# A PEER trunk kernel on one core: a group's one-hots in two VectorE instructions, two dots in front of them in every group, one set of dots beside each retrieval

## The reference, cut to what matters

```python
q = (hc @ wq).reshape(t, 8, 2, 128)
s = einsum("thpk,pnk->thpn", q, sk)                 # scores against 2 x 128 keys
s1, i1 = top_k(s[:, :, 0], 16); s2, i2 = top_k(s[:, :, 1], 16)
best, j = top_k(s1[..., :, None] + s2[..., None, :], 16)
e = i1[j // 16] * 128 + i2[j % 16]
gate = softmax(best)
act = gelu(einsum("thkd,td->thk", u_tab[e], hc))
out = einsum("thk,thkd->td", gate * act, v_tab[e])
```

## Time and profile before

| | us |
|---|---|
| median of 3 runs | 3139.86 (3136.67 to 3146.48) |
| profiled execution | 3141.54 |
| its span, first to last instruction | 3139.8 |
| busy: TensorE, VectorE | 2904.3 (93%), 2430.9 (77%) |
| busy: ScalarE, GpSimd | 1207.3 (38%), 1424.9 (45%) |
| mean granted TensorE clock | 0.975 of full |

### The profile page before, as it was taken

How to read it: one execution, slowest core, us unless ns; L and a number is a source line. 1 busy time by engine, 2 the same in 40 slices (tenths; PEclk the granted TensorE clock), 3 DMA queues, 4 the chain that set the end, 5 groups by cost and what they waited for, 6 DMA issues and landing times.

```text
span 3139.8 us, 50852 instructions
## 1 busy us (share of the span) xinstructions
PE 2904.3 (93%) x15754; PEld 2554.2 (81%) x15754; DVE 2430.9 (77%) x4532; ACT 1207.3 (38%) x1590; POOL 1424.9 (45%) x878
## 2 busy tenths in 40 slices
PE   5888999999998899999899899999999989999997
PEld 3657999989888788888777689989888878888885
DVE  7965679999995688888765307799999937888887
ACT  2333333345553333333333324333555523333332
POOL 2623367776667122222324244777766651222221
PEclk8999999999999999999999899999999989999998
DMA  6336567779898899999935124777788898999996
GB/s 240 134 128 221 199 206 240 242 263 349 308 350 321 301 353 350 355 356 352 351 122 174 66 100 138 229 251 239 277 328 328 310 348 308 352 353 351 357 347 232
DMA packets 352434, 849.74 MB, mean 271 GB/s; under 512 B 30048, under 2 KB 194016, under 8 KB 350176
## 3 DMA queue, kind: packets, MB, share of 16 engines
q1 hardware_dynamic: 239888, 479.53, 44.5%
q0 software_dynamic: 73728, 268.47, 23.6%
q10 hardware_dynamic: 38736, 100.84, 8.1%
HBM read 741.76 MB, written 106.95 MB: 270 GB/s over the span
## 4 chain that ended last, share of the span: by engine, by line
PE 54%; DVE 21%; issue 11%; POOL 7%; DMA 4%; ACT 1%; SPq 0%; POOLq 0%; DVEq 0%; ACTq 0%
PE bank L1418 11%; PE bank L1419 11%; PE bank L1420 11%; POOL w_lo L407 6%; DVE oh_c L995 5%; DVE oh_j L999 5%; PE bank L1360 4%; PE bank L1362 4%; PE bank L1361 4%; DVE rows L1160 2%; PE bank L1260 2%; PE bank L1262 2%; PE bank L1261 2%; DVE oh_i L996 2%; DMA x<-u_rows,u_idx 1%
## 5 line engine op out<-in xcount | busy, mean ns | idle before, releaser
L407 POOL TENSOR_TENSOR w_lo<-w_raw,w_hi 128x1024 fp32r<-128x1024 f32 x338 | 838.6, 2481 | 694.1 <-ACT w_hi L517 692.2
L517 ACT ACTIVATE w_hi<-w_raw 128x1024 fp32r<-128x1024 f32 x594 | 629.1, 1059 | 1346.3 <-PE bank L1420 668.6
L1360 PE MATMUL bank<-h_hi,w_hi 128*128 128x384 f32 x2048 | 702.7, 343 | 42.5 <-POOL w_lo L407 29.8
L1362 PE MATMUL bank<-h_lo,w_hi 128*128 128x384 f32 x2048 | 688.9, 336 | 0.0
L1361 PE MATMUL bank<-h_hi,w_lo 128*128 128x384 f32 x2048 | 688.3, 336 | 0.0
L461 POOL DMA_INDIRECT shared<-stream,v_idx x256 | 246.8, 964 | 830.9 <-DVE rows L1069 746.6
L1418 PE MATMUL bank<-w_hi,h_hi 128*128 128x512 f32 x1536 | 600.7, 391 | 16.6 <-ACT h_hi L642 14.3
L1419 PE MATMUL bank<-w_hi,h_lo 128*128 128x512 f32 x1536 | 600.0, 391 | 0.0
L1420 PE MATMUL bank<-w_lo,h_hi 128*128 128x512 f32 x1536 | 599.8, 390 | 0.0
L1039 DVE TENSOR_TENSOR w_lo<-w_raw,w_hi 128x1024 fp32r<-128x1024 f32 x256 | 313.7, 1226 | 199.9 <-ACT w_hi L517 199.0
L1360 PEld LDWEIGHTS bank<-h_hi,w_hi 128*128 128x128 f32 x2048 | 387.1, 189 | 58.9 <-issue 55.9
(11 more groups left out here) (193 smaller groups left out, 3584.6 us busy)
## 6 DMA issues: line engine op xcount, KB each, us to landing
w_raw<-stream SPq DMA_DIRECT2D x600, 512.0 KB
act_dram<-act_words ACTq DMA_DIRECT2D x256, 192.0 KB
gate_dram<-shared ACTq DMA_DIRECT2D x12, 4096.0 KB, 16.1
act_words<-act_dram SPq DMA_DIRECT2D x256, 192.0 KB
shared<-gate_dram SPq DMA_DIRECT2D x128, 384.0 KB
oh_j<-mod_rows SPq DMA_DIRECT2D x60, 512.0 KB, 4.7
oh_i<-mod_rows SPq DMA_DIRECT2D x20, 512.0 KB, 5.4
shared<-mod_rows SPq DMA_DIRECT2D x16, 512.0 KB, 14.0
```

Of the source, the lines that this page charges most:

```text
L407: nc.gpsimd.tensor_tensor(lo_of(grp, s), w_raw[:, s, :], hi_of(grp, s).bitcast(F32), ALU.subtract).then_inc(S["lo_ready"], 1)
L517: nc.scalar.activation(hi_of(grp, s), w_raw[:, s, :], ACT.Copy).then_inc(S["hi_ready"], 1)
L1360: MM(o, hi, h_hi[:, k, P:T], start=(k == 0), stop=False)
L1362: ins = MM(o, hi, h_lo[:, k, P:T], start=False, stop=(k == KC - 1))
```

## The change

It merges the two comparisons of a group into one instruction (`oh_i` and `oh_c` now lie in one tensor `oh_ic`, the keys of a group side by side in `keys_t`), and the three products into another (`gate_p` by group). In every group two dots come first, then the one-hots. The retrieval blocks keep the set of dots at their end and lose the other. GpSimd's fetch schedule follows: one fetch a tile for six tiles of a block; dots_to(g) changes from 36 + g + (g + 1) // 2 to 18 + 2g, and 14 dots are left behind the groups instead of 20.

```diff
-EARLY = 2 * DB * EARLY_SET
+EARLY = DB * EARLY_SET
 def dots_to(g):
-    return EARLY + g + (g + 1) // 2
+    return EARLY + 2 * g
...
-        oh_i = sb("oh_i", [P, 2, PAIR, NK, 2], BF16)
-        oh_c = sb("oh_c", [P, PAIR, NK, 2], BF16)
+        oh_ic = sb("oh_ic", [P, 3, PAIR, NK, 2], BF16)
+        oh_i, oh_c = oh_ic[:, 0:2, :, :, :], oh_ic[:, 2, :, :, :]
...
-        gate_p = key_words[:, 0:3 * DT].rearrange("p (a b) -> p a b", a=3)
-        i_t = key_words[:, 3 * DT:4 * DT]
-        j_t = key_words[:, 4 * DT:5 * DT]
+        gate_p = key_words[:, 0:3 * DT].rearrange("p (g w t) -> p g w t", w=3, t=GROUP)
+        keys_t = key_words[:, 3 * DT:5 * DT].rearrange("p (g w t) -> p g w t", w=2, t=GROUP)
...
                     if b < TB:
-                        end = 2 * (b - 1) * EARLY_SET + min(max(r - 1, 0), EARLY_SET) + (
-                            EARLY_SET if r == TILES_PER_BLOCK - 1 else max(r - 10, 0))
+                        end = (b - 1) * EARLY_SET + min(max(r - 2, 0), EARLY_SET)
                     elif group < GROUPS:
                         end = min(dots_to(max(group - 1, 0)) + U_RING, n + 2)
...
-                def early_dots(b, half):
+                def early_dots(b):
...
-                    early_dots(b, 0)
...
-                    V.tensor_copy(i_t[:, bass.ds(at, P)], ps[4][:, 0:P])
-                    V.tensor_copy(j_t[:, bass.ds(at, P)], ps[4][:, P:2 * P])
+                    for w in range(2):
+                        V.tensor_copy(keys_t[:, bass.ds((b - 1) * (P // GROUP), P // GROUP), w, :],
+                                      ps[4][:, w * P:(w + 1) * P].rearrange("p (g t) -> p g t", t=GROUP))
...
-                    early_dots(b, 1)
+                    early_dots(b)
...
                 def of_group(t, g):
-                    return t[:, g * GROUP:(g + 1) * GROUP].rearrange("p (a b) -> p a b", b=2).unsqueeze(2
-                                                                     ).to_broadcast([P, PAIR, NK, 2])
+                    n = t.shape[2]
+                    return t[:, g, :, :].rearrange("p n (a b) -> p (n a) b", b=2).unsqueeze(2
+                                                                   ).to_broadcast([P, n * PAIR, NK, 2])
                 def one_hots(g):
                     s = g % 2
-                    keys = iota_2[:].unsqueeze(1).to_broadcast([P, PAIR, NK, 2])
+                    keys = iota_2[:].unsqueeze(1).to_broadcast([P, 2 * PAIR, NK, 2])
...
-                    V.tensor_tensor(oh_c[:], keys, of_group(j_t, g), ALU.is_equal).then_inc(S["oh_cmp"], 1)
-                    V.tensor_tensor(oh_i[:, s, :, :, :], keys, of_group(i_t, g), ALU.is_equal)
+                    V.tensor_tensor(oh_ic[:, s:3:2 - s, :, :, :], keys, of_group(keys_t, g), ALU.is_equal
+                                    ).then_inc(S["oh_cmp"], 1)
                     dve.wait_ge(S["oh_cmp"], groups + g + 1)
-                    for w in range(3):
-                        ins = V.tensor_tensor(oh_j[:, s, w, :, :, :], oh_c[:], of_group(gate_p[:, w, :], g), ALU.mult)
-                    ins.then_inc(S["oh_ready"], 1)
+                    V.tensor_tensor(oh_j[:, s, :, :, :, :], oh_c.unsqueeze(1).to_broadcast([P, 3, PAIR, NK, 2]),
+                                    of_group(gate_p, g), ALU.mult).then_inc(S["oh_ready"], 1)
...
                 for g in range(GROUPS):
-                    one_hots(g)
                     for n in range(dots_to(g), dots_to(g + 1)):
                         dot(n)
+                    one_hots(g)
```

## The result

| | before | after |
|---|---|---|
| median, us | 3139.86 | 3234.97 (3 runs, 3231.94 to 3235.43) |
| ratio to before | | 1.030, 95% interval 1.0268 to 1.0324 |
| span of the profiled execution, us | 3139.8 | 3230.1 |

A forecast was written before the change was run, and what follows sets the result against it. TensorE held 54% of the last-ending chain and VectorE 21%, the latter from the groups. Retrieval -23, groups +99.6 and tail -12 sum to +65 on 3141.5, 3206; as median 3204 us, range 3112 to 3235.

The forecast's parts named there:

- The mechanism and its place: In the groups, the row fetched beside each 4 MB gate store comes late because fetch and use are closer; five stores a layer.
- The size of a store: In the groups, each store costs 10 us, between 3.3 and above 12.8; 50 us a layer.
- the next rows, 3 us or less apart, would be in time: In the groups, rows fetched after the late pair behind a store cause no further wait.
- Groups: Stage of 48 gating groups a layer: 339.5 us against 286.6 and 292.8, +52.9 and +46.7, both layers +99.6.
- The undisturbed step: In the groups away from stores, a pair goes from 12.48 to 12.36 us, 6.18 a group.
- The saving: In the groups, two one-hot instructions for five save net 0.12 us a pair: 3.01 becomes 2.89.
- Retrieval: Top-k blocks before the groups: one set of dots fewer beside each saves 11 us in layer 0, 12 in layer 1.
- less 3.6 for three blocks: In layer 0's retrieval, a block falls from 73.3 to 69.7 us, for three blocks alike, 11 us in all.
- Tail: Between groups and V stage, 10 rows remain instead of 15: -6 us a layer, between 0 and -11, both -12.
- One element per cycle: Rival: the merged one-hots' longer patterns run at 1.055 ns an element, 2.6 us more a pair, 3330 us; chance 0.03.
- rows in time: Rival: the row beside the store is ready by about 12.6 us into the step, no group waits, 3106 us; chance 0.15.
- balance: Rival: a store costs 3.3 us, replacing time VectorE is blocked by w_lo anyway; 3139 us, no change; chance 0.08.

## Why the prediction was right, point by point

*The mechanism and its place: right.* Fetch distance against the store's landing time decides. Shortening the distance alone makes the stall, spreading the store alone removes it, and the instants behind the first store are those forecast to a tenth of a microsecond at the cheap end.

*The size of a store: low by a tenth.* Forecast 10 us; the gaps above 47 x 6.18 - 1 = 289.5 come to 56.9 and 55.5 a layer, 11.4 and 11.1 a store. The stall itself was 9.4 (15.59 - 6.18), the low end of 9.3 to 10.4. The rest follows it: 0.7 to 2.2 in the next group (1.19 are lost on its 24 matmuls at the low clock), and 0.7 to 1.9 three or four groups on, where a row is late once more; one or two groups of 5.62 between give some of it back. The timeline behind the second store:

```profile
794.72 1.68 POOL L451 DMA_INDIRECT x<-u_rows,u_idx  x1 [2.05 <-DVE x L1003]
...
806.47 3.59 POOL L407 TENSOR_TENSOR w_lo<-w_raw,w_hi 128x1024 fp32r<-128x1024 f32 x1 [10.08 <-ACT w_hi L516]
...
810.21 1.83 POOL L451 DMA_INDIRECT x<-u_rows,u_idx  x1
...
817.06 1.22 DVE L1003 SCALAR_TENSOR_TENSOR x<-x,rows 128x1024 f32<-128x1024 f32 x1 [4.05 <-DMA x<-u_rows,u_idx]
```

The fetches stand behind w_lo of a tile, and no tile ends while TensorE is stalled: between 794.72 and 810.21 none is issued, and VectorE, which has caught up, waits for the row of 810.21. The forecast said that the next rows, 3 us or less apart, would be in time; that sentence failed for the rows wanted three or four groups on. Groups: +112 against a forecast of +99.6.

*The undisturbed step: right.* 6.12 and 6.25, 12.36 or so a pair, as forecast to the hundredth; one-hots of 1.22 and 1.76 unhindered (forecast 1.2 and 1.75) and 2.23 for the first when w_lo blocks it. That the hundredth fits is in part luck: GpSimd, of which the forecast has no step, is as close to the limit, with at most 0.17 us of waiting for w_hi before each w_lo from 690 to 709. The saving is a tenth of a microsecond a pair of groups, not the 0.47 estimated from the Trainium skill's formula (VectorE: DVE Perf Modes, TRN2 errata): three instructions fewer don't save three fixed parts here.

*Retrieval: the term that was mis-sized.* Forecast -23 for both layers, measured -7.1 and -8.1. Blocks 2 and 3 took 68.5, better than the 69.7 forecast. But block 1 gained nothing, and I had counted all three blocks alike. Without the first set of dots VectorE comes to the long top-k part some 23 us earlier (L918 at 452.59, in the kernel before L923 at 475.80), just where GpSimd issues block 1's fetches. The step that failed is "less 3.6 for three blocks"; a step that I had moved earlier has to be laid against what the other engines do at its new time.

*Tail: half.* Forecast -6 a layer, measured -5.0 and -1.7. I had read one tail, layer 0's, where the last V start was late; layer 1's was already 6 us shorter before.

*The rest.* One element per cycle, rows in time and balance are ruled out for the changed kernel by the durations and the 15 us spacings. The sum, -15 + 112 - 7 = 90, agrees with the spans; 95 by the medians, so the time came 31 us above the forecast. It is inside the range by 0.03 us, and that is luck: one of the three runs, 3235.43, lies outside. All three terms came out dearer than forecast: groups by 12 us, retrieval by 8, tail by 5.

## What to carry to other kernels

When work is moved ahead of a dependent step, count in steps of the loop how long a fetch has between issue and use, and lay that beside its slowest landing, not its usual one; a large store from another queue sets that landing. Cut such a store into pieces, and issue them one per step: alone that turned +3.0% into -0.4% here, with the dots behind the one-hots again into -1.4%. Reordering two items in a loop can be worth a whole step of slack.

## What the runs showed of the hardware

- A 512 KB gather issued just before a 4 MB store of 32,768-byte packets lands after 17.0 to 17.3 us, and the next one after 17.9 to 18.3 (ten stores on groups, changed kernel). Before the same store in 4,096-byte packets it is 9.0 to 10.6 and 9.5 to 11.1, and away from the stores 6.3 (median), 5.4 at best.
- Eight transfers issued in a row held ScalarE's queue for 9.12 us, where one took 0.34.
- An indirect fetch's issue on GpSimd takes 0.95 us alone, 1.23 beside VectorE's separate bf16 one-hots of 1024 elements, 1.76 and 1.47 beside the merged ones of 2048 and 3072, and 2.0 to 2.4 beside its long fp32 top-k operations.
